# A first modulation on TensorE during the preparation, and a first transition with one barrier

## What is computed

```python
cond = jax.nn.silu(c)
for i in range(DEPTH):                                   # DEPTH = 2
    mod = cond @ ada_w[i] + ada_b[i]                     # 1024 x 6144
    sh_t, sc_t, g_t, sh_c, sc_c, g_c = jnp.split(mod, 6, axis=-1)
    h = modulate(rms_norm(x, norm_g[i, 0]), sh_t, sc_t)
    h = s5_mixer(...) if i == 0 else diff_attention(...)
    x = x + g_t * rms_norm(h, norm_g[i, 1])
    h = modulate(rms_norm(x, norm_g[i, 2]), sh_c, sc_c)
    h = conv_ffn(h, ffn_w_in[i], ffn_conv_w[i], ffn_conv_b[i], ffn_w_out[i])
    x = x + g_c * rms_norm(h, norm_g[i, 3])
```

## Time and profile before

| | us |
|---|---|
| runs (three) | 1428.3, 1431.76, 1436.23 |
| median | 1431.76 |
| profiled execution | 1425.57 |
| its span | 1423.8 |
| TensorE busy | 1275.9 |
| VectorE busy | 861.3 |
| ScalarE busy | 498.1 |
| GpSimd busy | 423.9 |

### The profile page before, as it was taken

The page is one execution under the profiler, slowest core; times in us unless marked ns, Lnnn a source line. Parts: engine busy times, 40 slices in busy tenths (PEclk is TensorE's granted clock), DMA queues, the critical chain, the costliest instruction groups (busy, mean ns, idle before and its releaser), DMA issues.

```text
span 1423.8 us, 17367 instructions
## 1 busy us (share of the span) xinstructions
PE 1275.9 (90%) x6250; PEld 1010.5 (71%) x6250; DVE 861.3 (60%) x1107; ACT 498.1 (35%) x749; POOL 423.9 (30%) x273
## 2 busy tenths in 40 slices
PE   5632699979999999999899999987989999999995
PEld 1322588868888888888678667665768888888884
DVE  8999868658988544324683566664775444443223
ACT  2153242224433334223331444333534334432311
POOL 3992012124454333200022423320024443341001
PEclk9665799959999999999899999987989999999997
DMA  8002978704766422323223213120113232223311
GB/s 333 1 1 38 166 284 310 265 1 152 291 244 251 154 89 88 119 89 118 71 78 115 60 45 89 44 74 30 59 34 114 90 116 89 88 93 114 109 69 60
DMA packets 35430, 164.97 MB, mean 116 GB/s; under 512 B 4528, under 2 KB 14000, under 8 KB 17200
## 3 DMA queue, kind: packets, MB, share of 16 engines
q1 hardware_dynamic: 34368, 163.97, 33.9%
q10 hardware_dynamic: 1008, 0.27, 0.1%
HBM read 156.95 MB, written 3.08 MB: 112 GB/s over the span
## 4 chain that ended last, share of the span: by engine, by line
PE 78%; DVE 15%; issue 2%; DMA 2%; SPq 1%; ACT 1%; DVEq 0%; ACTq 0%; POOL 0%; POOLq 0%
PE psum L1736 16%; PE psum L1737 16%; PE psum L1738 16%; PE psum L1866 5%; PE psum L1867 5%; PE psum L1868 5%; PE psum L1924 3%; PE psum L1620 2%; PE psum L1948 1%; PE psum L1927 1%; PE psum L1810 1%; SPq L375 1%; PE psum L1909 1%; PE psum L1910 1%; PE psum L1911 1%
## 5 line engine op out<-in xcount | busy, mean ns | idle before, releaser
L1736 PE MATMUL psum<-hhi,whi 128*128 128x512 f32 x960 | 382.8, 399 | 6.6 <-DVE hlo L1373 3.4
L1737 PE MATMUL psum<-hlo,whi 128*128 128x512 f32 x960 | 377.1, 393 | 0.0
L1738 PE MATMUL psum<-hhi,wlo 128*128 128x512 f32 x960 | 377.0, 393 | 0.0
L1185 DVE TENSOR_TENSOR wlo<-raw,whi 128x2048 fp32r<-128x2048 f32 x82 | 200.1, 2440 | 171.8 <-ACT whi L691 171.8
L691 ACT ACTIVATE whi<-raw 128x2048 fp32r<-128x2048 f32 x81 | 155.2, 1916 | 179.8 <-PE psum L1868 146.1
L1736 PEld LDWEIGHTS psum<-hhi,whi 128*128 128x128 f32 x960 | 182.4, 190 | 49.1 <-issue 9.4
L567 POOL TENSOR_TENSOR ca<-ca,cb 128x512 f32<-128x512 f32 x44 | 136.9, 3111 | 249.9 <-ACT ca L801 249.9
L1738 PEld LDWEIGHTS psum<-hhi,wlo 128*128 128x128 f32 x960 | 182.2, 190 | 38.8
L1737 PEld LDWEIGHTS psum<-hlo,whi 128*128 128x128 f32 x960 | 182.4, 190 | 36.1
L1401 DVE SCALAR_TENSOR_TENSOR ca<-psum,convp,ca 128x511 f32<-128x511 f32 x44 | 32.9, 748 | 200.0 <-ACT ca L797 199.9
L1866 PE MATMUL psum<-ghi,whi 128*128 128x512 f32 x352 | 137.2, 390 | 1.5 <-DVE wlo L1185 1.5
(11 more groups left out here) (342 smaller groups left out, 1783.9 us busy)
## 6 DMA issues: line engine op xcount, KB each, us to landing
raw<-in_units SPq DMA_DIRECT2D x92, 1024.0 KB, 4.8
ada_ring<-in_ada_w SPq DMA_DIRECT2D x40, 1024.0 KB, 4.9
ada_raw<-in_ada_w SPq DMA_DIRECT2D x8, 1024.0 KB, 14.4
toep<-toeplitz_rows SPq DMA_DIRECT2D x32, 128.0 KB, 8.9
qk_sw<-ca SPq DMA_DIRECT2D x32, 128.0 KB, 2.3
u<-in_x_blocks SPq DMA_DIRECT2D x1, 2048.0 KB, 14.0
x<-in_x_t SPq DMA_DIRECT2D x1, 2048.0 KB, 9.4
out_t<-x SPq DMA_DIRECT2D x8, 256.0 KB, 2.0
```

Source lines behind the costliest of these rows:

```text
L1185: TT(wlo[:, s, :], raw[:, s, :], whi[:, s, :].bitcast(F32), ALU.subtract).then_inc(split_lo, 1)
L1736: M(out, w_hi, hi[:, k, :], start=(k == 0), stop=False)
L1737: M(out, w_hi, lo[:, k, :], start=False, stop=False)
L1738: return M(out, w_lo, hi[:, k, :], start=False, stop=(k == KT - 1))
```

## The change

The first layer's modulation now goes through TensorE whole: 24 units instead of 8. Units 0 to 7 use the five slots, the others two slots by turns. The four matmuls of a unit write to partitions 0, 32, 64 and 96 of one bank (four column groups) and not to partition 0 of four banks. A third (8 units) is copied by ScalarE (`copy_row`) and turned by 16 small matmuls (`turn_row`). Units 8 to 15 stand ahead of the transposes of `lb`, units 16 to 23 between them, the second and third `turn_row` behind the matmul that signals `umod_psum`. VectorE takes up the modulation (`modulation(0, (2, 3, 4, 5))`) at the end of its output powers.

In the gated linear unit VectorE does one `ada_step` per unit, now for layer 1, adds squares of the old x, and makes the three sums. GpSimd's sum is gone. TensorE sums x's squares (`stat_x`) ahead of unit 7. The first half of the second MLP unit is split before unit 7 ends (`first_half_high`, `first_half_low`). The first transition is `barrier(0)` with `next_input(0)`, in the form of the others, and both MLPs begin alike: TensorE goes through the input tiles once for one and a half units. The other 16 `ada_step` of layer 1 are spread over bodies 0 to 11: one, two, one per body in groups of four bodies. TensorE's reductions stand before bodies 2, 8 and 12. All semaphore counts of later stages move accordingly. The diff, cut to its core:

```diff
--- before.py
+++ after.py
@@ -57,7 +57,7 @@
 U_QK = U_V + N_V
 U_WO = U_QK + N_QK
 N_UNITS = U_FOUT[1] + N_FOUT
-N_ADA_PE = KT
+N_ADA_PE = 3 * KT
 N_ADA0 = 5
...
@@ -351,8 +347,9 @@
         def _(sp):
             sp.dma_start(s5s[:, 0:3, :], a["s5_par"]).then_inc(par_in, 16)
             def load_ada0(n):
-                wait(sp, ada_used, n + 1 - N_ADA0)
-                sp.dma_start(ada0_raw[:, n % N_ADA0, :], a["ada_w"][n]).then_inc(ada0_landed[n % N_ADA0], 16)
+                wait(sp, ada_used, n + 1 - N_ADA0 if n < KT else n - 2 if n < KT + 2 else n - 1)
+                slot = ada0_slot(n)
+                sp.dma_start(ada0_raw[:, slot, :], a["ada_w"][n]).then_inc(ada0_landed[slot], 16)
...
@@ -399,19 +396,25 @@
                 sp.dma_start(ada_ring[:, s, :], a["ada_w"][m + N_ADA_PE]).then_inc(ada_landed[s], 16)
 
             sp.wait_ge(y5_psum, OCTS)
+            load_unit(2, 0, None)
+            load_unit(3, 1, None)
             load_ada(0, 0)
             load_ada(1, 1)
-            load_unit(2, 0, None)
-            load_unit(3, 1, None)
+
+            def load_one(i, s, half):
+                load_ada(i + 2, s)
+                load_unit(i + 4, s, half)
 
             def load_both(i, s, half):
-                load_ada(2 * i + 4, 0)
+                load_ada(2 * i - 10, 0)
                 load_unit(i + 4, s, half)
-                load_ada(2 * i + 5, 1)
-
-            load_ada(2, 0)
-            load_ada(3, 1)
-            pairs(sp, 0, N_GLU + 10, load_both)
+                load_ada(2 * i - 9, 1)
+
+            pairs(sp, 0, N_GLU + 4, load_one)
+            pairs(sp, N_GLU + 4, N_GLU + 8, load_both)
+            for i in range(N_GLU + 8, N_GLU + 10):
+                load_ada(i + 6, i % 2)
+                load_unit(i + 4, i % 2, None)
...
@@ -656,14 +635,24 @@
             for i, lb in enumerate((lb_re, lb_im)):
                 A(lb[:, :, 0, :], bb[:, i], ACT.Copy).then_inc(row0_ready, 1)
 
-            act.wait_ge(ada_used, N_ADA_PE)
-            A(mod_row[:].rearrange("p (b k) -> p b k", b=4), psum[0:1, 0:4, :], ACT.Copy).then_inc(row_copied, 1)
+            def copy_row(third):
+
+                act.wait_ge(ada_used, KT * third + KT)
+                if third == 2:
+                    act.wait_ge(mod0_psum, 1)
+                for b in range(4):
+                    ins = A(sq[32 * b:32 * b + 1, third % 2, :], psum[32 * b:32 * b + 1, third % 2, :], ACT.Copy)
+                ins.then_inc(row_copied, 1)
+
+            act.wait_ge(usq_added, 8)
+            copy_row(0)
             for t in range(16):
                 act.wait_ge(inb_psum, t + 1)
-                if t == 8:
-                    act.wait_ge(mod0_psum, 1)
                 dst = (inb_re if t < 8 else inb_im)[:, 4 * (t % 8):4 * (t % 8) + 4, :]
                 A(dst, psum[:, 2 + t % 2, :].rearrange("p (g k) -> p g k", g=4), ACT.Copy).then_inc(inb_ready, 1)
+                if t == 8:
+                    copy_row(1)
+            copy_row(2)
...
+            def x_square(f):
+
+                act.wait_ge(x_in, 16)
+                wait(act, xsq_added, f - 2 if f > 2 else 0)
+                A(x_sq[:, f % 2, :] if f else x_sum[:], x[:, f, :], ACT.Square).then_inc(xsq_ready, 1)
+
+            def glu_squares(f):
+
+                y, g = y_glu[:, f, :], gate[:, 0, f:f + 1]
+                act.wait_ge(y_ready, f + 1)
+                wait(act, sum_a, f - 2 if f > 2 else 0)
+                A(sq[:, f % 2, :] if f else ssum[:], y, ACT.Square).then_inc(sqa_ready, 1)
+                wait(act, sum_c, f - 2 if f > 2 else 0)
+                A(glu_sq[:, f % 2, :] if f else cb[:, 1, :], y, ACT.Square, scale=g).then_inc(sqc_ready, 1)
+                act.wait_ge(sqc_ready, f + 1)
+                A(y, y, ACT.Copy, scale=g).then_inc(yg_ready, 1)
...
+                if i < N_GLU - 1:
+                    split_high(i + 2, s, i // 2 + 1)
+                    if i == 0:
+                        x_square(0)
+                    x_square(i + 1)
+                if i == 0:
+                    act.wait_ge(mod_read, 1)
+                glu_squares(i)
+
+            def first_half_high(n0, after, count):
+
+                act.wait_ge(raw_landed[1], 16 * (n0 // 2 + 1))
+                act.wait_ge(after, count)
+                A(whi[:, 1, 0:UNIT // 2], raw[:, 1, 0:UNIT // 2], ACT.Copy).then_inc(half1_hi, 1)
+
+            def second_half_high():
+
+                A(whi[:, 1, UNIT // 2:], raw[:, 1, UNIT // 2:], ACT.Copy).then_inc(split_hi, 1)
+
+            for i in range(N_GLU - 1):
+                glu(i, i % 2)
+            first_half_high(U_FIN[0], glu_half, 1)
+            glu(N_GLU - 1, 1)
...
@@ -1169,6 +1157,9 @@
             signal(cl_dve)
             dve.wait_ge(cl_pool, 2 * len(POOL_CL))
             dve.wait_ge(row0_ready, 4)
+            dve.wait_ge(mod_psum, 2)
+            modulation(0, (2, 3, 4, 5))
+            signal(mod_read)
...
+                if r == 0:
+                    dve.wait_ge(stat_x, 1)
+                    link(nc.vector.tensor_copy(stat[:, 24:24 + QT], psum[:, 5, 0:QT]))
+                dve.wait_ge(stat_a, r + 1)
...
                 if layer == 0:
-                    for third in range(3):
-                        dve.wait_ge(acc_clear, (4, 4, 5)[third])
-                        pairs(dve, 4 * third, 4 * third + 4, partial(body, third=third))
+                    pairs(dve, 0, 4, partial(body, first=lambda j, s, half: ada_step(
+                        j + KT, s, half + KT // 2 + 1, j, 1)))
+                    dve.wait_ge(acc_clear, 3)
+                    pairs(dve, 4, 8, partial(
+                        body, first=lambda j, s, half: ada_step(2 * j + (KT - 4), 0, j + 3, j, 1),
+                        second=lambda j, s, half: ada_step(2 * j + (KT - 3), 1, j + 3, j - 4, 0)))
+                    pairs(dve, 8, 12, partial(body, first=lambda j, s, half: ada_step(
+                        j + (KT + 4), s, half + 7, j - 4, 0)))
                     pairs(dve, 12, 16, body)
...
+            def glu(i, s):
+                dve.wait_ge(sig_ready, i + 1)
+                TT(y_glu[:, i, :], psum[:, 2 * s, :], ca[:, s, :], ALU.mult).then_inc(y_ready, 1)
+                if i < N_GLU - 1:
+                    split_low(i + 2, s, None)
+                    x_square_add(i + 1)
+                    ada_step(i, s, i // 2 + 1, i, 0)
+                tile_sums(0, i)
+
+            for i in range(N_GLU - 1):
+                glu(i, i % 2)
+            first_half_low(0)
+            ada_step(N_GLU - 1, 1, 4, N_GLU - 1, 0)
+            glu(N_GLU - 1, 1)
+            next_input(0, {KT - 1: lambda: second_half_low(0)})
             ffn(0)
             next_input(1, {4: lambda: split_low(U_V + 1, 1, None)})
...
-            def ada_unit(k, s):
-
-                pe.wait_ge(ada0_landed[s], 16 * (k // N_ADA0) + 16)
+            def ada_unit(n):
+
+                third, k = divmod(n, KT)
+                pe.wait_ge(ada0_landed[ada0_slot(n)], ada0_count(n))
+                if k == 0:
+                    wait(pe, row_copied, third - 1)
                 for b in range(4):
-                    ins = M(psum[0:1, b, :], cond[:, 1, k:k + 1], ada0_raw[:, s, 512 * b:512 * b + 512],
+                    ins = M(psum[32 * b:32 * b + 1, third % 2, :], cond[:, 1, k:k + 1],
+                            ada0_raw[:, ada0_slot(n), 512 * b:512 * b + 512],
                             start=(k == 0), stop=(k == KT - 1))
                 ins.then_inc(ada_used, 1)
+
+            def turn_row(third):
+
+                pe.wait_ge(row_copied, third + 1)
+                if third:
+                    pe.wait_ge(mod_psum if third > 1 else mod0_psum, 1)
+                for b in range(4):
+                    rows = slice(32 * b, 32 * b + 1)
+                    for q in range(4):
+                        f = THIRD * third + 4 * b + q
+                        ins = M(psum[:, 7, f:f + 1], sq[rows, third % 2, P * q:P * q + P], ones[rows, 0:1],
+                                start=True, stop=True)
+                    if b < 3:
+                        ins.then_inc(row_turned, 1)
+                        pe.wait_ge(row_turned, 3 * third + b + 1)
+                ins.then_inc(mod_psum if third else mod0_psum, 1)
 
             def reduce_acc(slot, col0):
...
             pe.wait_ge(cond_ready, 1)
-            for n in range(N_ADA_PE):
-                ada_unit(n, n % N_ADA0)
+            for n in range(KT):
+                ada_unit(n)
...
-            pe.wait_ge(row_copied, 1)
-            for f in range(THIRD):
-                ins = M(psum[:, 7, f:f + 1], mod_row[0:1, P * f:P * f + P], ones[0:1, 0:1],
-                        start=True, stop=True)
-            ins.then_inc(mod0_psum, 1)
+            turn_row(0)
+            for n in range(KT, 2 * KT):
+                ada_unit(n)
             pe.wait_ge(lb_pool, 2 * len(POOL_LB))
             pe.wait_ge(lb_dve, 1)
             pe.wait_ge(row0_ready, 4)
@@ -1644,9 +1625,13 @@
```

(59 more changed lines are left out.)

297 lines of the change are left out of this document (80 added, 217 removed).

## The result

The kernel before takes 1431.69 us (median of six runs, 1428.3 to 1436.23), the changed one 1443.91 us (1439.69 to 1447.52): ratio 1.0087, 95% interval 1.007 to 1.0104. It is slower. The profiled execution took 1442.14 us around a span of 1440.3, against 1425.57 and 1423.8: 16.5 us more in the spans, 12.2 in the medians.

What follows compares the result with a forecast made beforehand. TensorE was taken as the bound, with 78% of the chain of waits. Terms -23.9 + 8.6 + 24.1 + 3 = +11.8 on the median 1431.76 gave 1443.6 us, range 1433 to 1454, slower at 72%.

Steps and rivals of the forecast that it cites:

- Transition: From last gated linear unit matmul to first MLP matmul: 41.4 us becomes 17.5, a gain of 23.9; bounds 19.4 to 25.2.
- (d): End of the gated linear unit: VectorE is late, the stretch to the MLP takes 22 us, total 1448; chance 9%.
- Gated linear unit: TensorE stands 5.5 us ahead of unit 7, then runs at a fallen clock: +8.6 us, bounds 6.4 and 9.5.
- First MLP: TensorE idles 12.0 and 6.1 us before second and third reductions, which then run slowly: +24.1 us, bounds 18.3 and 26.
- each of three reductions costs 5.3 us: First MLP of the kernel before: 3.5 us for the reduction itself, the rest the clock after it.
- lower bound of 18.3 us: First MLP loss if the clock stayed high, each of the two reductions taking 3.5 us.
- Preparation: Sixteen more modulation units on TensorE: umod near 102 us, last output power 130.6 instead of 127.7, +3; bounds +1, +14.
- (a): First MLP: TensorE's waits are already met when it comes to them; 24.1 us off, 1419.5, change faster; chance 7%.
- (b): Three new TensorE idle times: the clock does not fall, 6 + 2 us less, near 1435.5, no change; chance 14%.
- (c): Preparation: column groups do not overlap or loads land late; 11 us more, 1454.6; chance 10%.

Runs made afterwards that it cites:

- the second profile: The changed kernel as it is, run once more beside the kernel before on the same chip: 1447.09 us, ratio 1.013.

## Why the prediction was right, step by step

**Transition**, -23.9 predicted, -23.5 measured (17.9 us against 17.5). Built from the earlier trace rows it stood within its bounds; rival (d), VectorE late at the end of the unit, did not occur here only because the stall ahead of unit 7 had cleared VectorE's queue. When the stall was taken away it did: 19.85 us, in between.

**Gated linear unit**, +8.6 predicted, +8.9 measured: idle 5.4 (5.5), four matmuls 1.87 us (1.7), half pace afterwards 1.5 (1.4).

**First MLP**, +24.1 predicted, +25.7 measured. Idle 11.8 (12.0) and 6.2 us (6.1), reductions 6.98 and 6.99 us (6.9). That 12.0 came so near is partly luck: the same wait was 12.8 us in the second profile. The sequence on VectorE after the end of body 7, in the timeline of all engines, is the one of the earlier trace rows:

```profile
402.12 0.78 ACT L785 ACTIVATE ca<-psum,convp 128x512 f32<-128x512 f32 x1 [0.24 <-PE psum L1725]
...
405.82 2.34 DVE L1239 SCALAR_TENSOR_TENSOR ada_acc<-ada_ring,cond,ada_acc 128x2048 f32<-128x2048 f32 x1
...
408.08 2.28 DVE L1176 TENSOR_TENSOR wlo<-raw,whi 128x2048 fp32r<-128x2048 f32 x1
...
410.28 3.34 DVE L1239 SCALAR_TENSOR_TENSOR ada_acc<-ada_ring,cond,ada_acc 128x2048 f32<-128x2048 f32 x1
```

That a reduction slows the body behind it even when its wait was met, the prediction had read rightly from the earlier trace rows. Two sizes were wrong, and their errors partly cancel. The pace of the bodies afterwards was taken too low: 3.0 and 2.1 us lost, not 1.4 each. And "each of three reductions costs 5.3 us" in the kernel before holds for two of them. The third, with no idle time ahead of it, took 4.47 us, and the body behind it lost 2.5, near 6.8 us together:

```profile
482.66 4.47 PE L1620 MATMUL psum<-ones,ada_acc 128*128 128x1 f32 x32
```

The lower bound of 18.3 us, for a clock that stays up, doesn't follow from its own terms either: with 3.5 for each of the two reductions they give 17.3, with 5.3 for a reduction and its body 18.1.

**Preparation**, +3 predicted, +3.6 measured, partly by another way, so that its nearness is luck in part. umod came at 99.7, not 102: seven of the sixteen units met the high clock (1.04 us) where I took the low one for all. VectorE's last output power ended at 129.45 (before 127.68; I had 130.6), +1.8, and the first toeplitz store moved by as much (131.01 to 132.79), under the 2 to 4 us that I gave. The third piece of the toeplitz product starts 4.2 us later, at 177.56 instead of 173.36: 2.4 us more arise on the way, where TensorE waits for the gathered rows, and 0.6 come back behind it.

```profile
177.56 3.60 PE L1664 MATMUL psum<-toep,u 128*64 128x128 f32 x32 [9.06 <-DMA toep<-toeplitz_rows]
```

I had taken this stretch as unchanged. Which part of the change slows it, no run tells (last section). Over nine profiles with the changed preparation and four column groups, with umod where it was or earlier, the start lies between 190.5 and 194.1 us, against 188.7 and 188.9 in the two profiles with the old one.

The estimate by the Trainium skill ("TensorE: Matmul & The Clock Gate", Part 3, "Measured speedup vs the span model", 2.38 times for three column groups) had put a unit at 2.2 us and umod near 105. Four groups with 512 columns measured 3.59 / 1.04 = 3.5 times the pace of one, a unit 1.89 us at the low clock, and umod came at 99.7; no run here has three groups.

**Rivals.** (a) fell: the waits were not met, and they cost what was forecast; it would have been true two bodies later. (b) fell for the reductions (6.98 us, granted clock 0.50). Its price was about right: without the idle time the two reductions and the bodies behind them take 6.8 us less (5.9 + 0.9, reductions two bodies later) where I had put 6, and in the unit the slow matmuls and the half pace cost 0.9 and 1.5 us where I had put 2. Filling the waits gave back only 3.8, since the reductions lost the high clock on the way all the same. (c) fell: the groups overlap. (d) is told above.

**The total.** 1443.6 against 1443.91 is closer than the method is: the profiled spans differ by 16.5 us and not by 11.8, the second comparison gives 1.013, and the terms were each 0.3 to 1.6 us off, all in one direction, 2.9 us together. The profiled execution itself was forecast at 1437.4 us and took 1442.14. What the forecast had right is the sign, the waits that decide it, and each size to within 1.6 us.

## What to carry to other kernels

A wait in an in-order queue should be priced by what stands ready behind it, and by where the awaited step stands in the *other* engine's queue: here "the newest result of the body just computed" cost 12 us, the same result asked for two bodies later nothing. When a sequence is shortened, look at which small steps were moved ahead of a matrix stage to pay for it, and put them behind it instead. And after a stall is removed, look at the next queue: what had used the stall as cover (an accumulation of 2.34 us) comes into the open and can be moved in turn.

## What the runs showed of the hardware

A run of 32 one-column matmul records leaves TensorE at half pace for 7 to 12 of the following matmuls even when it was preceded and followed by dense work (1.5 to 2.5 us lost, over the kernels whose reductions in the MLP found no idle time). With no idle time ahead of it such a run takes 3.6 to 4.7 us; after 6.2 us of idle time and after 11.8 it takes 6.98 to 6.99 us.

The gather of the toeplitz rows is slower with the changed preparation. SyncE needs longer to issue its last 16 transfers, here in the kernel before and in the changed one:

```profile
152.14 19.89 SPq L375 DMA_DIRECT2D toep<-toeplitz_rows  x16
```

```profile
153.49 22.77 SPq L372 DMA_DIRECT2D toep<-toeplitz_rows  x16
```

It is 19.9 and 19.6 us in the two profiles with the old preparation and 21.1 to 23.8 in the ten with the changed one. From the end of the last output power to the start of the third piece of the product it is 45.7 and 45.4 us against 46.3 to 49.2. The bytes per second in the middle of the gather don't tell the two apart (last column; the DMA share before it hardly differs). The same stretch in the kernel before, with reductions two bodies later, and with filled waits:

```profile
168.00:173.00 5.00, 0.00 (x0) 0.00 (x0) 5.00 (x6) 0.00 (x0) 0.00 (x0) 0.82 1.28 130
```

```profile
168.00:173.00 5.00, 1.42 (x50) 1.28 (x44) 4.96 (x7) 0.54 (x2) 0.00 (x0) 1.00 1.28 112
```

```profile
168.00:173.00 5.00, 0.00 (x0) 0.00 (x0) 5.00 (x7) 0.00 (x0) 0.00 (x0) 0.99 1.24 137
```

130 and 129 GB/s stand in the profiles with the old preparation, 112 to 137 in those with the changed one. The transfers of this stretch and their order are the same. The cause stays open.
